# Second attention block of a two-block kernel: one product for both row maxima, factor rows stored in token order, low parts ahead of convolution taps in three steps

## What is computed

```python
q, k, v, u, g = project(h, w_in, q_g, k_g)      # 8 query heads, 2 key heads, width 128
s = einsum('bqkgd,bskd->bkgqs', q, k) * 128 ** -0.5   # 256 context + 512 own keys
p = softmax(s, axis=-1)
attn = einsum('bkgqs,bskd->bqkgd', p, v)
y_b = silu(layer_norm(depthwise_conv(a * sigmoid(b), dw_w, dw_b)))  # 31 taps, 512 channels
x = x + (sigmoid(g_a) * (attn @ w_attn_out) + sigmoid(g_b) * (y_b @ w_conv_out)) @ w_out
```

## Time and profile before

| | |
|---|---|
| median of three runs | 1599.19 us |
| the profiled execution's own time | 1599.78 us |
| its span, first to last instruction | 1597.9 us |
| TensorE matmul busy | 99% of the span |
| VectorE busy | 69% of the span |
| ScalarE busy | 45% of the span |
| granted TensorE clock | 1.000 |
| second attention, from the first scores to `attn_out` | 930.6 to 1108.9 us |

### The profile page before, as it was taken

The page is one execution under the profiler, slowest core; times in us unless marked ns, Lnnn a source line. Parts: engine busy times, 40 slices in busy tenths (PEclk is TensorE's granted clock), DMA queues, the critical chain, the costliest instruction groups (busy, mean ns, idle before and its releaser), DMA issues.

```text
span 1597.9 us, 21908 instructions
## 1 busy us (share of the span) xinstructions
PE 1579.5 (99%) x7852; PEld 1319.9 (83%) x7852; DVE 1108.9 (69%) x1804; ACT 721.5 (45%) x1238; POOL 173.8 (11%) x190
## 2 busy tenths in 40 slices
PE   9999999999999999999999999999999999999998
PEld 7888888888888888888878888887879888888887
DVE  7676998886688765655775889998667553443446
ACT  5545776765442222323552654446434432332234
POOL 0121300000400000000007960000000000000000
PEclk9999999999999999999999999999999999999999
DMA  5566512214545556543232222122422333332333
GB/s 174 181 179 182 142 54 60 67 61 144 223 139 173 211 183 211 172 143 93 79 119 92 82 71 58 55 67 59 139 93 67 106 105 92 93 105 92 94 103 106
DMA packets 50402, 186.44 MB, mean 117 GB/s; under 512 B 7096, under 2 KB 8888, under 8 KB 47888
## 3 DMA queue, kind: packets, MB, share of 16 engines
q1 hardware_dynamic: 39024, 135.96, 26.8%
q0 software_dynamic: 10608, 48.60, 9.7%
q10 hardware_dynamic: 688, 0.79, 0.2%
HBM read 175.83 MB, written 6.87 MB: 114 GB/s over the span
## 4 chain that ended last, share of the span: by engine, by line
PE 88%; DVE 8%; ACT 2%; issue 1%; DMA 1%; SPq 0%; DVEq 0%; ACTq 0%
PE ps L2297 19%; PE ps L2298 19%; PE ps L2299 19%; PE ps L2380 2%; PE ps L2381 2%; PE ps L2382 2%; PE ps L2572 2%; PE ps L2574 1%; PE ps L2573 1%; PE ps L2846 1%; PE ps L2845 1%; PE ps L2847 1%; PE ps L2531 1%; PE ps L2903 1%; DVE w_lo L1324 1%
## 5 line engine op out<-in xcount | busy, mean ns | idle before, releaser
L2297 PE MATMUL ps<-h_hi,w_hi 128*128 128x512 f32 x832 | 326.8, 393 | 1.1 <-DVE h_lo L1938 0.7
L2299 PE MATMUL ps<-h_hi,w_lo 128*128 128x512 f32 x832 | 324.0, 389 | 0.0
L2298 PE MATMUL ps<-h_lo,w_hi 128*128 128x512 f32 x832 | 323.8, 389 | 0.0
L1324 DVE TENSOR_TENSOR w_lo<-raw,w_hi 128x1024 fp32r<-128x1024 f32 x178 | 222.3, 1250 | 77.1 <-ACT w_hi L705 65.0
L638 ACT ACTIVATE w_hi<-raw 128x1024 fp32r<-128x1024 f32 x125 | 131.4, 1052 | 166.6 <-DMA raw<-in_panels 166.6
L2297 PEld LDWEIGHTS ps<-h_hi,w_hi 128*128 128x128 f32 x832 | 156.2, 188 | 37.0 <-issue 2.5
L2299 PEld LDWEIGHTS ps<-h_hi,w_lo 128*128 128x128 f32 x832 | 156.1, 188 | 32.8
L2298 PEld LDWEIGHTS ps<-h_lo,w_hi 128*128 128x128 f32 x832 | 156.2, 188 | 32.5 <-issue 0.7
L2297 PE MATMUL ps<-f_hi,w_hi 128*128 128x512 f32 x408 | 159.4, 391 | 0.0
L2299 PE MATMUL ps<-f_hi,w_lo 128*128 128x512 f32 x408 | 158.8, 389 | 0.0
L2298 PE MATMUL ps<-f_lo,w_hi 128*128 128x512 f32 x408 | 158.8, 389 | 0.0
(11 more groups left out here) (459 smaller groups left out, 3278.2 us busy)
## 6 DMA issues: line engine op xcount, KB each, us to landing
raw<-in_panels SPq DMA_DIRECT2D x250, 512.0 KB, 3.5
wm<-in_w_mod POOLq DMA_DIRECT2D x16, 1536.0 KB, 6.8
scratch_r<-scratch_t POOLq DMA_DIRECT2D x8, 320.0 KB, 5.1
kd<-k_hi POOLq DMA_DIRECT2D x16, 128.0 KB, 3.0
kd<-k_lo POOLq DMA_DIRECT2D x16, 128.0 KB, 3.3
bias<-scratch_c POOLq DMA_DIRECT2D x8, 256.0 KB, 3.7
bias<-scratch_r POOLq DMA_DIRECT2D x8, 256.0 KB, 3.0
X<-in_x POOLq DMA_DIRECT2D x1, 2048.0 KB, 8.4
```

The costliest lines, as they stand in the source:

```text
L1324: dve.tensor_tensor(w_lo[:, n % RING], raw[:, n % RING], w_hi[:, n % RING].bitcast(F32), ALU.subtract)\
L2297: pe.matmul(out, w_hi[:, u, b, :], hi[:, k, :N], start=start, stop=False)
L2298: pe.matmul(out, w_hi[:, u, b, :], lo[:, k, :N], start=False, stop=False)
L2299: ins = pe.matmul(out, w_lo[:, u, b, :], hi[:, k, :N], start=False, stop=stop)
```

## The change

Three edits. In `row_max2` both reductions come first, then one wait and one product over two columns, which counts one semaphore step in place of two. The factor tile is stored in HBM in token order (element (q, t) at 128 t + q, so every float is a run of its own), the load is as before, and `o_norm` reads and writes with step one. In steps 13, 14 and 15 the tap of place 0 stands behind the low parts of pairs 0 and 1 instead of ahead of them.

```diff
-    scratch_f = nc.dram_tensor("scratch_f", (H2, P, NT), F32).ap()
+    scratch_f = nc.dram_tensor("scratch_f", (H2, T), F32).ap()
...
-            gp.dma_start(scratch_f[h], factor[:, h % 2, :]).then_inc(sem("rows_stored"), 16)
+            gp.dma_start(bass.AP(tensor=scratch_f.tensor, offset=h * T, ap=[[1, P], [P, NT]]), factor[:, h % 2, :], allow_slow_non_contiguous=True).then_inc(sem("rows_stored"), 16)
...
-            act.wait_ge(sem("neg_max2"), 2 * w + 2)
+            act.wait_ge(sem("neg_max2"), w + 1)
...
-        def row_max2(w, e):
+        def row_max2(w):
             if w < UNITS:
                 dve.wait_ge(sem("qk2_done"), 2 * w + 2)
-                h, t, m = w // 2, 2 * (w % 2) + e, neg_max[:, w % 2, e:e + 1]
-                chain(dve.tensor_reduce(m, s2(e), AX, ALU.max, negate=True))
-                dve.tensor_tensor(m, m, q_r[:, h, t:t + 1], ALU.mult).then_inc(sem("neg_max2"), 1)
+                h, t, m = w // 2, 2 * (w % 2), neg_max[:, w % 2, 0:2]
+                for e in range(2):
+                    ins = dve.tensor_reduce(neg_max[:, w % 2, e:e + 1], s2(e), AX, ALU.max, negate=True)
+                chain(ins)
+                dve.tensor_tensor(m, m, q_r[:, h, t:t + 2], ALU.mult).then_inc(sem("neg_max2"), 1)
...
-            dve.tensor_tensor(by_token(o_n[:]), by_token(ps[:, 6 + h % 2, :]),
-                              r_row[h % 2][:].rearrange("p (q t) -> p t q", t=NT), ALU.mult).then_inc(sem("o_normed"), 1)
+            dve.tensor_tensor(o_n[:], ps[:, 6 + h % 2, :], r_row[h % 2][:], ALU.mult).then_inc(sem("o_normed"), 1)
...
         for w in range(UNITS + 2):
-            taps_at(w, 0) if w < UNITS else None
+            taps_at(w, 0) if w <= 12 else None
             lo_turn2(w - 1, 0)
             lo_turn2(w - 1, 1)
+            taps_at(w, 0) if 12 < w < UNITS else None
             if w == UNITS:
                 o2_lo(H2 - 2)
                 taps_at(w, 0)
-            row_max2(w, 0)
-            row_max2(w, 1)
+            row_max2(w)
```

More of the change, by code:

```diff
@@ L2054, in factor2_of @@
             dve.reciprocal(factor[:, h % 2, :], row_sum[:, h % 2, :]).then_inc(sem("o_factor"), 1)
-        def by_token(t):
-            return t.rearrange("p (t q) -> p t q", q=P)
         def o_norm(h):
```

## The result

| | before | changed |
|---|---|---|
| median | 1599.29 us (6 runs, 1598.8 to 1599.51) | 1605.97 us (6 runs, 1604.59 to 1607.06) |
| profiled execution, its span | 1599.78, 1597.9 us | 1606.74, 1605.0 us |
| granted TensorE clock | 1.000 | 0.997 |
| first scores to `attn_out` | 178.26 us | 176.99 us |

The ratio is 1.0042, with an interval of 1.0032 to 1.0052: slower by 0.4%, where 1597.0 was forecast. The second attention did become shorter, by 1.27 us. All of the loss lies behind it, within some 12 us.

A forecast was written before the change was run, and what follows sets the result against it. TensorE was taken to set the pace, VectorE counting only where TensorE waits. Gains of 1.3 + 0.2 + 0.7 = 2.2 us took the profiled 1599.78 to 1597.6, less 0.6 for the median: 1597.0, range 1595.4 to 1599.0.

The forecast's parts named there:

- the bound of the store: Factor store to HBM in 512 four-byte runs: lands after 2.5 to 3.5 us, bounds 1.7 and 6.8, costed at nothing.
- rival 4: Head 7's store delays TensorE in `attn_out`, us for us past 4.6; 0.2% slower from 10 us (1602.4); chance 0.04.
- some 5.1: Sum in us of TensorE's late restarts in the second attention; with 1.2 of others, at most 6.3 to gain.
- the second rival: Its name for the Trainium skill's objection to the factor store: one descriptor per element, no duration given for four bytes.
- rivals 3 and 4: 3: restarts stay, `o_norm` no faster or store slow, 1598.0 to 1602.4, chance 0.14; 4: head 7's store makes it slower, 0.04.
- The pair of maxima: VectorE, first reduction to the tap behind the pair: 1.94 us in place of 2.14, gaining 0.20 per unit, bounds 0.07 and 0.30.
- Step 0: First step's maxima product, perhaps held by GpSimd's sum: nothing taken, up to 0.5 us as the other end.
- `o_norm`: Multiplication by the factor row, read with step one: 0.69 us in place of 1.08, gaining 0.39 for each of eight heads.
- No late product of pair 2 in steps 3 to 13: TensorE's late starts in odd steps 3 to 11 all go, 1.3 us; step 13's lateness of 0.22 goes too.
- Steps 0 to 2: Start of the second attention: 0.2 us from step 1's maxima, nothing taken for its first step.
- Steps 13 to 16: One chain held by the maxima: gains 0.7 us, not 1.4; step 16's first product becomes late by about 1.4.
- Rival 2: Maxima don't hold steps 14 and 15, and step 0 gives its part: gain 3.4 us, 1595.8; chance 0.12.

The follow-up runs named there:

- the fillers: Changed kernel plus 26 unread matmuls ahead of factor k = 7 in `attn_out`: 1610.13 us when they ran twice, 1604.06 us in the first panel only.
- the first kernel with fillers: Changed kernel plus 26 unread matmuls ahead of factor k = 7, which ran again later in `attn_out`: 1610.13 us, ratio 1.0067.
- the second kernel with fillers: Changed kernel plus 26 unread matmuls ahead of factor k = 7 in the first `attn_out` panel only: 1604.06 us, ratio 1.0032.
- the third kernel with test stores: Kernel before plus seven unused GpSimd test stores in various forms, each issued after its head's row load landed; landings 1.7 to 10.2 us, no kernel time given.
- the three good versions: Kernel before with maxima and tap edits only, 1597.41 us; changed kernel with head 7's old store and multiplication, 1597.16; changed kernel with 8-byte runs, 1597.63.

## Why the prediction was wrong

**The step that failed** is the bound of the store: "Bounds: 1.7 (number of runs free) and 6.8 (all of it grows fourfold). I take 2.5 to 3.5". The store landed after 8.3 to 10.8, outside both. The upper end had one model in it, a time in proportion to the number of runs, and the table above shows that this model is wrong: the price was the neighbourhood of the writes, which no row of before had. Its own sentence "no row has such short runs" should have left the upper end open. With it the chance of rival 4 was too small: its "10 us is six times the store before" is an argument from size, not from a row.

**Rival 4's mechanism and its price came true.** It said that the store may take 2.9 longer before TensorE is late, and from there one for one. The last store took 10.78, 9.1 more than 1.7; 9.1 less 2.9 is 6.2, and TensorE was 6.12 late, at the factor k = 7 of the first `attn_out` panel, as said. That the two agree to 0.1 is in part luck: the row load of head 7 took 3.55 in place of 4.1 (its median over the heads rose to 5.2), while TensorE was due 12.20 behind the store's issue in place of 12.64. The rival put the point of 0.2% at 10 us; its price for a store of 10.78 would be 1597.0 and 6.2, 1603.2, and what is missing to the measured 1605.97 is mostly the next point.

**A term was missing.** No case had a price for what TensorE does after a stall. It was 2.2 to 2.3 us, shown by the fillers. More than a third of what the stall itself cost came on top.

**The DMA rule of the Trainium skill** (DMA: Bandwidth & Descriptors, Rules for kernel authors), that a strided last dimension goes out as one descriptor for each element, spoke against this edit, and rightly in its direction. But the number of descriptors that it names is not what cost the time: 512 separate floats that are spaced landed about as soon as 128 runs of 16 bytes. Nor does the count of packets in the profile show them: 50402 in both kernels.

**Two slips that change nothing.** The latenesses that the prediction lists add up to 4.9 us, not to "some 5.1", so that the most that all waits and restarts hold is 6.1 and not 6.3. And the slow store, which it calls "the second rival" beside the Trainium skill, stands in its rivals 3 and 4.

**The rest of the working held.**

- The pair of maxima: 1.94 forecast, 1.93 measured; 16 products, 0.16 where nothing disturbs them.
- Step 0 gives nothing, as taken. The product took 0.67 and ended with GpSimd's sum, and did so in all seven kernels with the new product, within 0.03: 937.06 and 937.03 here, 936.27 and 936.25 with maxima and tap, 936.21 and 936.20 with the maxima alone. By the Trainium skill (SBUF — State Buffer, Who interferes with whom) the one issued second is held until the first is done; these rows agree.
- `o_norm`: 0.69 forecast, 692 ns measured.
- No late product of pair 2 in steps 3 to 13: TensorE's restarts there are gone. From the scores of step 2 to those of step 13, 1.3 was forecast; the version with the old last head gained 1.32, the changed kernel only 0.52. The difference is not in any wait: a step of TensorE with the same instructions took 11.16 us in this execution and in two others (with the fillers in the first panel only, with runs of eight bytes), and 11.09 in the even steps before and in the version with the old last head. It isn't the change: the first kernel with fillers has the changed one's instructions up to `attn_out`, took 11.09 and gained 1.33. So it goes with the execution; what sets these 0.07 per step stays open, and no wait shows it.
- Steps 0 to 2: 0.2 forecast, 0.14 to 0.21 in five of the versions, 0.01 in the changed kernel's profile, and 0.10 lost in that of the second kernel with fillers. In these two VectorE came to the maxima of step 0 later: their product ended 6.27 and 6.35 us behind the first scores, against 5.62 before. TensorE waited 0.7 and 0.8 for an exponential, of which the shorter step 1 gave back the larger part. This isn't the change either: the third kernel with test stores, whose maxima are the old ones, does the same (6.35, a wait of 0.8), and the first kernel with fillers doesn't (5.62).
- Steps 13 to 16: 0.7 forecast, not 1.4; 0.74 measured. What was to be late next is late: the first product of step 16 by 1.46 ("about 1.4"), with the exponentials of steps 14 and 15 released by the product of the maxima. Rival 2 falls.
- The whole, without the failed term: 1597.0 forecast, 1597.16 measured with the last head's old store. That this is so close has some luck in it, for the medians of the three good versions differ by 0.5.

## What to carry to other kernels

A transfer whose form stands in no row has no upper bound from the rows of other forms: measure that one form by itself, or keep it off the head or tile whose cover is a few us, and put it where the cover is long. Few bytes say nothing of a store's time; floats written one by one side by side into HBM took five to six times as long as the same floats in runs of 16 bytes (medians of 9.6 and 10.2 against 1.7 us), and runs of 8 bytes with a read step of two gave the fast read and most of the fast store. When a stall of TensorE of several us is priced, the slower clock behind it belongs to the price.

## What the runs showed of the hardware

- Neighbouring 4-byte writes from SBUF to HBM, issued by GpSimd: 7.0 to 11.9 us for 0.5 to 2 KB, against 1.7 to 3.2 in runs of 16 bytes, 3.1 to 5.8 in runs of 8 bytes, and 1.7 to 2.3 for floats 16 bytes or more apart. Right behind a load of 256 KB the fast forms took 5.1 and 5.4.
- GpSimd's issue of the store rose from 0.545 to 0.762 us with the new form, 0.72 with runs of 8 bytes.
- VectorE reads a float32 row from SBUF with a step of two at the speed of step one (692 ns for 128 x 512), and with a step of four in 1076.
- After 6 us of idle time inside a busy stretch TensorE was granted 0.50 and 0.61 in the two next stretches of 3 us, and 1.00 after that; with 26 matmuls in the gap it stayed at 1.00.
- Open: whether another queue than GpSimd's writes the short runs as slowly, for which there is no run; the length of the stretch in which writes collide; and the step of 11.09 or 11.16 us.
